# Modulation slices moved to other units, first value products by pairs of k-tiles, and gated attention scores by levels, in a hybrid transformer block

## The chip, the cores and the metric

The kernel runs on one core of one Trainium2 chip. The metric is the device time of one execution in microseconds (us); the median of several executions counts. One further execution was recorded by the hardware profiler; its trace is what the rows below come from. Engines are named as in the profile: PE is TensorE (matmuls), PEld its weight loads, DVE is VectorE, ACT is ScalarE, POOL is GpSimd, SP is SyncE, which issues most of the DMAs in program order.

## The reference, cut to what matters

One block over 512 tokens of width 1024, all in float32:

```
mod = silu(c) @ ada_w + ada_b                  # 1024 x 6144: shift1, scale1, gate1, shift2, scale2, gate2
h   = rmsnorm(x) * (1 + scale1) + shift1
gq, gk, gv, gr, g_lr, aq, ak, av, merge_a, merge_b = split(h @ w_in)
log_a = log_sigmoid(g_lr @ w2 + bias) / 16
# gated linear attention, 4 heads, dk 128, dv 256, chunks of 16 tokens
#   within a chunk: (q e^b)(k e^-b)^T, causal; across chunks: a state decayed by e^b_last
y_gla  = (rmsnorm(o_gla) * silu(gr)) @ w_gla
y_attn = dilated_attention(aq, ak, av) @ w_attn       # 12 heads of 64, rotary
x = x + gate1 * ((sigmoid(merge_a) * y_gla + sigmoid(merge_b) * y_attn) @ w_out)
h2 = rmsnorm(x) * (1 + scale2) + shift2
x = x + gate2 * (conv_ffn(h2) @ w_down)
out = rmsnorm(x)
```

## The kernel before, in words

**Products.** Every large product is made of three matmuls in a reduced float32 form: both operands are split into a high and a low part, and high x high, high x low and low x high are summed in PSUM (`three`, L1641). Weights come in units of 1 MB (`UNITS`, L95): two value units for the wide value heads (`vw`), six `qk`, `lr`, then for each of four heads `gqk`, `gv`, `gr`, then `ma`, `mb`, `wa`, `wg`, `wo`. Each unit is read by DMA into one of two slots of `raw`; ACT writes the high part (`split_hi`, L584), DVE the low part (`split_lo`, L1084), which frees the slot through the semaphore `raw_used`. A unit gives mostly two tiles of 128 x 512; the two PSUM banks 0 and 1 take turns by the position in `TILES`.

**Modulation.** shift1 and scale1 are needed first. `ada_in` holds their 8 MB in four quarters j; DVE sums 8 rows for each j (`ada_sums`, L1042), PE adds over the partitions with one-column matmuls (`shift_scale`, L1663), DVE makes the gain (`shift_and_gain`), ACT the high part of h (`high`) and DVE the low (`lower`). The other 16 slices (two groups r of 8) pass through the same two slots of `raw` as the weights, in the order of `RAW` (L125), and DVE adds each to `ada_acc` (`modulate`, L1110). When a group is summed, 16 one-column matmuls on 128-wide weights (`ada_part`, L1723) are strewn into one ordinary tile, named in `WITH_ADA`: group 0 in the second tile of the last `qk` unit, group 1 in the second tile of `gr` of head 2. The sums take a bank of their own in the alternation and DVE empties it (`ada_tile`).

**First products.** PE's order is written out at L1963: transposes of x, then the narrow value product (`first_hi`, `first_lo`, banks 0 and 1) and the wide one. The wide one takes k-tiles 0 to 3 together in `wide_hi(r)` after the third pair's modulation has begun, `wide_lo(k)` later, and k-tiles 4 to 7 at the very end, in `wide_rest`.

**Dilated attention.** While the second three `qk` units run, pieces of the attention of the first two heads are put between the tiles (`attention(p, i)`, PE L1797, DVE L1207). DVE also rotates each `qk` tile out of its bank (`rotate`, L1147), and SP carries the rotated halves to `qk` in eight DMAs (`shuffle`, L453), which stand in SP's queue between the weight loads, as do eight small copies of the gate weights (L493, L496).

**Gated attention.** For head h, steps `gla(h, i)` are put between the tiles of the next head. Step 0: PE sums the logs of the gates over chunks into two banks (128 columns and, in `side[1]`, 9 columns for each block of 128 tokens), ACT takes exponentials, DVE scales k and q. For each block b of 128 tokens DVE makes eight copies of the keys, each decayed up to one chunk further (`keys`, L1265: one copy of 128 x 1024 and eight multiplications in a row), and PE makes the scores from eight matmuls of 16 columns, each with its own copy as weights (`within`, L1842, L1852). `outputs` (L1856) then adds the values and the state.

Of the kernel before, what the change touches and what calls it, by code (L numbers as in the profile page):

```python
# [16 lines left out]
P = 128  # L17
# [37 lines left out]
C_KEEP = C_TRI + P + NCH + 1  # L55
# [18 lines left out]
def shape_constants():  # L74
# [6 lines left out]
    for n in range(NCH + 1):  # L81
        c[:, C_TRI + P + n] = np.where(row[:, 0] < CHUNK * n, -1.0 / 16.0, 0.0)
# [30 lines left out]
WITH_ADA = {(("qk", 1, 2), 1): 0, (("gr", 2, 0), 1): 1}  # L113
# [38 lines left out]
LATE = KT - 2  # L152
SPLIT_K = 5

def hybrid_block_kernel(nc, x, c, positions, ada_w, ada_b, norm1_w, w_in, gate_w2, gate_b, gla_norm_w,
# [3 lines left out]
    with ctx:  # L160
# [28 lines left out]
        def region(*places):  # L189
# [35 lines left out]
        q_in, k_in, gv, gr, logs, za, lrT, w2s, og_hi, og_lo, kk, at_sb, kt_sb, ke, state, eb, enb, ed, qB, o_sb, osq, ors = region(  # L225
# [4 lines left out]
            ("kk", 88, [P, NCH, P], F32), ("at_sb", 92, [P, 2, P], F32), ("kt_sb", 93, [P, 2, P], F32),  # L230
            ("ke", 94, [P, P], F32), ("state", 94.5, [P, DV], F32), ("eb", 95.5, [P, SEQ], F32),
            ("enb", 97.5, [P, SEQ], F32), ("ed", 99.5, [P, NB, NCH + 1], F32), ("qB", 99.75, [P, SEQ], F32),
            ("o_sb", 101.75, [P, 2, SEQ], F32), ("osq", 105.75, [P, 2, SEQ], F32), ("ors", 109.75, [P, SEQ], F32))

        vx_hi, vx_lo = region(("vx_hi", 16, [P, UE], F32R), ("vx_lo", 24, [P, UE], F32R))

# [63 lines left out]
        b_ps, gexp_done, qg_done, qB_done, kk_step, kk_done = (sem(n) for n in (  # L300
            "b_ps", "gexp_done", "qg_done", "qB_done", "kk_step", "kk_done"))
# [89 lines left out]
        def _(sp):  # L391
# [83 lines left out]
            for q in range(N_RAW):  # L475
# [5 lines left out]
                if q == 3:  # L481
# [3 lines left out]
                    sp.wait_ge(mod1_ps, KT // 2)  # L485
# [92 lines left out]
        def _(act):  # L578
# [91 lines left out]
            normed_out(4)  # L670
            normed_out(5)
            modulated(0)
            modulated(1)
            normed_out(6)
            normed_out(7)
            split_hi(1)
            for k in (2, 3):
                high(k)
            for k in (2, 3):
                modulated(k)  # L680
            for k in (4, 5):
                high(k)
            for k in (4, 5):
                modulated(k)
            split_hi(2)
            for k in (6, 7):
                high(k)

# [73 lines left out]
            def gla(h, i):  # L762

                if i == 0:
                    act.wait_ge(b_ps, h + 1)
                    if h > 0:
                        act.wait_ge(kk_done, NB * h)
# [3 lines left out]
                    act.activation(ed[:, :, :].rearrange("p b n -> p (b n)"), side[1][:, 0:NB * (NCH + 1)],  # L771
# [79 lines left out]
            for n in range(GROUPS):  # L851
                if n == 2:
                    split_hi(n + 1)
# [179 lines left out]
        def _(dve):  # L1033
# [8 lines left out]
            def ada_sums(j, half):  # L1042
# [4 lines left out]
                for k in range(half * KT // 2, (half + 1) * KT // 2):  # L1047
                    if k == 0:
                        dve.tensor_scalar(total, total, c_silu[:, 0:1], None, ALU.mult).then_inc(ada_step, 1)
                    else:  # L1050
                        dve.wait_ge(ada_step, KT * j + k)
# [58 lines left out]
            def modulate(n):  # L1110

                if n >= 2 * KT:
                    return
# [151 lines left out]
            def keys(h, b):  # L1265

                u = NB * h + b
                if u >= 1:
                    dve.wait_ge(at_ps, u)
                    dve.wait_ge(kk_done, u)  # L1270
                own = k_in[:, h % 2, b * P:(b + 1) * P]
                dve.tensor_copy(kk[:, :, :], own.rearrange("p (a n) -> p a n", a=1).broadcast_to((P, NCH, P))).then_inc(kk_step, 1)
                for n in range(NCH):
                    w = CHUNK * (n + 1)
                    decay = eb[:, b * P + w - 1:b * P + w]
                    dve.wait_ge(kk_step, NCH * u + n + 1)
                    dst = kk[:, n + 1, 0:w] if n < NCH - 1 else ke[:, :]
                    dve.tensor_scalar(dst, kk[:, n, 0:w], decay, None,
                                      ALU.mult).then_inc(kk_step if n < NCH - 1 else kk_done, 1)

            def gla(h, i):

                if i == 0:
# [9 lines left out]
                    keys(h, 0)  # L1293
                    chunks = q.rearrange("p (b n c) -> p b n c", b=NB, n=NCH)
                    start = ed[:, :, 0:NCH].rearrange("p b (n o) -> p b n o", o=1).broadcast_to((P, NB, NCH, CHUNK))
                    dve.tensor_tensor(qB[:, :].rearrange("p (b n c) -> p b n c", b=NB, n=NCH), chunks, start,
                                      ALU.mult).then_inc(qB_done, 1)
                if 2 <= i <= 5:
# [7 lines left out]
                    if b + 1 < NB:  # L1306
                        keys(h, b + 1)
                if 3 <= i <= 5:
                    b = i - 3
                    dve.wait_ge(p3_done, NB * h + b + 1)  # L1310
                    new = side[1][:, 64:64 + DV]
# [4 lines left out]
                    else:  # L1316
                        dve.wait_ge(st_done, 3 * h + b)
                        ins = dve.scalar_tensor_tensor(state[:, :], state[:, :], ed[:, b, NCH:NCH + 1], new,
# [56 lines left out]
            split_lo(0)  # L1375
            ada_sums(1, 0)
# [4 lines left out]
            split_lo(1)  # L1381
            ada_sums(2, 0)
            ada_sums(2, 1)
            lower(2)
            lower(3)
            shift_and_gain(2)
            ada_sums(3, 0)
            ada_sums(3, 1)
            lower(4)
            lower(5)  # L1390
            shift_and_gain(3)
            for k in (6, 7):
                modulate_late(k)
            for k in (6, 7):
                lower(k)
            split_lo(2)
            modulate(0)

            def evac_wide():
# [795 lines left out]
```

## Time and profile before

| | |
|---|---|
| median of 3 executions | 958.49 us (958.16 to 959.00) |
| profiled execution, its own time | 959.86 us |
| its span, first to last instruction | 958.1 us |
| instructions | 12161 |
| PE busy | 920.2 us (96%) |
| DVE busy | 527.1 us (55%) |
| ACT busy | 372.7 us (39%) |

The span is what the trace shows; the time of the execution holds 1.8 us more around it. The profiled execution is 1.4 us over the median. In rows of instructions the columns are start, duration, engine, line of the code, operation, tiles written and read, shapes and count; in square brackets is how long the engine stood idle before and what ended it. A matmul of plain float32 is recorded as two instructions, one in the reduced form as one.

### The profile page before, as it was taken

How to read it: one execution, taken by the hardware profiler on the slowest of the kernel's cores; microseconds unless marked ns; L12 is line 12 of the kernel's file. 1: busy time of each engine (PE TensorE's matmuls, PEld its weight loads, DVE VectorE, ACT ScalarE, POOL GpSimd, SP SyncE). 2: the span in 40 equal slices, each digit the busy share in tenths (PEclk: the TensorE clock that was granted, in tenths of full speed). 3: DMA queues.
4: the chain of work that ended last, by engine and by line, in shares of the span. 5: the costliest groups of instructions: out<-in, count | busy, mean ns of one | idle time of the engine just before them, and what ended most of it. 6: DMA issues, size and time to landing. Idle time of an engine off the chain costs nothing.

```text
span 958.1 us, 12161 instructions
## 1 busy us (share of the span) xinstructions
PE 920.2 (96%) x4733; PEld 781.5 (82%) x4733; DVE 527.1 (55%) x687; ACT 372.7 (39%) x461; POOL 35.9 (4%) x33
## 2 busy tenths in 40 slices
PE   3899999999999999999999999999999999999996
PEld 3887787889989898888888788888888888888885
DVE  5877893775756365653254466555555555433223
ACT  5451112568443334625223335343333433422225
POOL 0010000000000000000002120000000000000003
PEclk9999996999999999999999999999999999999999
DMA  9947844723441212122222442333343333322302
GB/s 312 382 133 224 245 113 111 241 89 105 160 132 45 75 59 75 58 88 75 101 88 88 176 114 63 88 88 88 107 112 88 88 88 104 116 88 99 120 0 88
DMA packets 114270, 112.87 MB, mean 118 GB/s; under 512 B 4676, under 2 KB 104390, under 8 KB 111927
## 3 DMA queue, kind: packets, MB, share of 16 engines
q1 hardware_dynamic: 113511, 110.16, 36.7%
q10 hardware_dynamic: 720, 2.16, 0.6%
q8 instruction: 28, 0.46, 0.2%
q14 instruction: 11, 0.09, 0.0%
HBM read 104.77 MB, written 4.19 MB: 114 GB/s over the span
## 4 chain that ended last, share of the span: by engine, by line
PE 84%; DVE 6%; DMA 3%; ACT 2%; SPq 2%; issue 2%; DVEq 0%; ACTq 0%
PE bank L1644 23%; PE bank L1646 23%; PE bank L1645 23%; PE bank L1852 2%; DMA raw<-in_w_in_dram 2%; PE bank L2106 1%; ACT w_hi L593 1%; SPq L461 1%; PE bank L1727 1%; DVE w_lo L1092 1%; DMA x<-x_spill 1%; PE bank L1939 1%; PE bank L1793 1%; PE bank L1873 1%; PE bank L1766 1%
## 5 line engine op out<-in xcount | busy, mean ns | idle before, releaser
L1644 PE MATMUL bank<-h_hi,w_hi 128*128 128x512 f32 x672 | 269.1, 400 | 8.2 <-DVE w_lo L1092 5.2
L1646 PE MATMUL bank<-h_hi,w_lo 128*128 128x512 f32 x672 | 263.6, 392 | 0.0
L1645 PE MATMUL bank<-h_lo,w_hi 128*128 128x512 f32 x672 | 263.2, 392 | 0.0
L1644 PEld LDWEIGHTS bank<-h_hi,w_hi 128*128 128x128 f32 x672 | 127.3, 189 | 35.8 <-issue 8.8
L1646 PEld LDWEIGHTS bank<-h_hi,w_lo 128*128 128x128 f32 x672 | 127.1, 189 | 27.0
L1645 PEld LDWEIGHTS bank<-h_lo,w_hi 128*128 128x128 f32 x672 | 127.3, 189 | 25.4 <-issue 0.2
L1092 DVE TENSOR_TENSOR w_lo<-raw,w_hi 128x2048 fp32r<-128x2048 f32 (+2 forms) x46 | 85.6, 1872 | 60.8 <-ACT w_hi L593 56.1
L1099 DVE TENSOR_TENSOR w_lo<-raw,w_hi 128x2048 fp32r<-128x2048 f32 x31 | 71.1, 2292 | 86.3 <-ACT w_hi L601 86.3
L1598 DVE SCALAR_TENSOR_TENSOR conv<-bank,vecs,conv 128x511 f32<-128x511 f32 x88 | 65.7, 748 | 65.8 <-ACT conv L984 60.3
L593 ACT ACTIVATE w_hi<-raw 128x2048 fp32r<-128x2048 f32 (+2 forms) x44 | 71.7, 1644 | 60.3 <-DMA raw<-in_w_in_dram 52.0
L601 ACT ACTIVATE w_hi<-raw 128x2048 fp32r<-128x2048 f32 x31 | 59.1, 1905 | 69.3 <-PE bank L1646 69.3
L984 ACT ACTIVATE conv<-bank,vecs 128x512 f32<-128x512 f32 x44 | 34.1, 778 | 104.7 <-PE bank L1646 104.7
L1644 PE MATMUL bank<-hs_hi,w_hi 128*128 128x512 f32 x176 | 68.6, 390 | 0.0
L1646 PE MATMUL bank<-hs_hi,w_lo 128*128 128x512 f32 x176 | 68.5, 389 | 0.0
L1645 PE MATMUL bank<-hs_lo,w_hi 128*128 128x512 f32 x176 | 68.5, 389 | 0.0
L1646 PEld LDWEIGHTS bank<-hs_hi,w_lo 128*128 128x128 f32 x176 | 33.0, 188 | 6.9
L1644 PEld LDWEIGHTS bank<-hs_hi,w_hi 128*128 128x128 f32 x176 | 33.0, 188 | 6.9
L1645 PEld LDWEIGHTS bank<-hs_lo,w_hi 128*128 128x128 f32 x176 | 33.0, 188 | 6.7
L1644 PE MATMUL bank<-w_hi,h_hi 128*128 128x256 f32 x128 | 36.5, 285 | 0.1
L1645 PE MATMUL bank<-w_lo,h_hi 128*128 128x256 f32 x128 | 36.2, 283 | 0.0
L1646 PE MATMUL bank<-w_hi,h_lo 128*128 128x256 f32 x128 | 36.2, 283 | 0.0
L1125 DVE SCALAR_TENSOR_TENSOR ada_acc<-raw,c_silu,ada_acc 128x2048 f32<-128x2048 f32 x14 | 32.9, 2347 | 3.1 <-DMA raw<-in_ada_w_dram 2.9
(267 smaller groups left out, 1345.1 us busy)
## 6 DMA issues: line engine op xcount, KB each, us to landing
raw<-in_w_up_dram SPq DMA_DIRECT2D x44, 512.0 KB, 4.7
raw<-in_w_in_dram SPq DMA_DIRECT2D x19, 1024.0 KB, 5.2
raw<-in_ada_w_dram SPq DMA_DIRECT2D x16, 1024.0 KB, 5.5
raw<-in_w_down_dram SPq DMA_DIRECT2D x22, 512.0 KB, 3.6
raw<-in_w_in_dram SPq DMA_DIRECT2D x20, 512.0 KB, 5.2
ada_in<-in_ada_w_dram SPq DMA_DIRECT2D x16, 512.0 KB, 9.6
raw<-in_w_gla_branch_dram SPq DMA_DIRECT2D x4, 1024.0 KB, 4.9
raw<-in_w_out_dram SPq DMA_DIRECT2D x4, 1024.0 KB, 6.2
```

Source lines behind the costliest of these rows:

```text
L461: sp.dma_start(qk[32 * half:32 * half + 32, g, a // 2, a % 2, :], rope[32 * a:32 * a + 32, j % 2, half, :]).then_inc(qk_in[j % 2], 16)
L593: last = act.activation(hv, r, ACT.Copy)
L601: act.activation(w_hi[:, slot, :], raw[:, slot, :], ACT.Copy).then_inc(hi_done, 1)
L984: act.activation(conv[:, s, t, :], bank[2 * (1 - s) + t][:, :], ACT.Identity, scale=vecs[:, bass.ds(i + (V_CW2 + t * FT), 1)], bias=vecs[: ...
L1092: last = dve.tensor_tensor(lv, r, hv.bitcast(F32), ALU.subtract)
L1099: dve.tensor_tensor(w_lo[:, slot, :], raw[:, slot, :], w_hi[:, slot, :].bitcast(F32), ALU.subtract).then_inc(raw_used, 1)
L1125: ins = dve.scalar_tensor_tensor(ada_acc[:, :], src, c_silu[:, k:k + 1], ada_acc[:, :], ALU.mult, ALU.add)
L1598: ins = dve.scalar_tensor_tensor(conv[:, s, t, tap:SEQ], src[:, 0:SEQ - tap], vecs[:, bass.ds(i + (col + t * FT), 1)], conv[:, s, t, tap:S ...
L1644: pe.matmul(out_ap, wh, xh, start=first, stop=False, skip_group_check=True)
L1645: pe.matmul(out_ap, wh, xl, start=False, stop=False, skip_group_check=True)
L1646: return pe.matmul(out_ap, wl, xh, start=False, stop=last, skip_group_check=True)
L1852: pe.matmul(side[2][0:m, at:at + CHUNK], kk[:, n, 0:m], q_in[:, h % 2, b * P + at:b * P + at + CHUNK], start=True, stop=True, skip_group_c ...
```

## The change

1. The 16 late slices of the modulation are tied to other units (`ADA_UNITS`): the first three `qk`, then `gqk`, `gv`, `gr` of head 1, `gqk`, `gv` of head 2, all three of head 3, the four `ma` and the first `mb`. `WITH_ADA` moves too: group 0 goes into the second tile of `gr` of head 2, group 1 into the second tile of the last `mb`; `ada_tile(0)` and `ada_tile(1)` move with them.
2. The first products go in quarters of two k-tiles: `quarter_hi(j)` (narrow and wide, both high parts), `shift_scale(j + 1)`, `quarter_lo(j)`. `wide_rest` is gone. The first six transposed tiles stand ahead of `shift_scale(0)` instead of four. In quarter 1 the last of the eight rows isn't summed by DVE; PE multiplies it by the column of `c_silu` (`DIRECT`). The splits of the units 1, 2 and 3 stand earlier on ACT and DVE, and SP's order of loads is another: both value units ahead of the second quarter of `ada_in`, the spill of x after the load of unit 3.
3. The eight decayed key copies of each block are replaced by scaled copies made once for each head (`scaled_copies`): seven broadcast multiplications by factors from 45 columns of chunk sums for each block, instead of 9. Scores of a block: two matmuls over every second chunk (the even ones with the keys as they are, the odd ones with `mixed` keys), two on pairs of 32 columns, one on a half of 64 columns, five in place of eight.

```diff
-WITH_ADA = {(("qk", 1, 2), 1): 0, (("gr", 2, 0), 1): 1}
+WITH_ADA = {(("gr", 2, 0), 1): 0, (("mb", 3, 0), 1): 1}
+ADA_UNITS = ([("qk", 0, g) for g in range(GROUPS)] + [(kind, 1, 0) for kind in ("gqk", "gv", "gr")]
+             + [("gqk", 2, 0), ("gv", 2, 0)] + [(kind, 3, 0) for kind in ("gqk", "gv", "gr")]
+             + [("ma", u, 0) for u in range(4)] + [("mb", 0, 0)])
+ADA_AT = {UNIT[u]: n for n, u in enumerate(ADA_UNITS)}
 for _n in range(N_UNITS):
     RAW.append(("w", _n))
-    if _n == 2:
-        RAW.append(("ada", 0))
-    if _n == 3:
-        RAW += [("ada", 1), ("ada", 2)]
-    if 4 <= _n <= 2 * KT:
-        RAW.append(("ada", _n - 1))
+    if _n - 1 in ADA_AT:
+        RAW.append(("ada", ADA_AT[_n - 1]))
...
-            for j in range(KT // 2):
-                if j in (1, 2):
-                    load(j - 1)
-                load_first(j)
+            load_first(0)
+            load(0)
+            load(1)
+            load_first(1)
+            load_first(2)
             load(2)
+            load_first(3)
+            load(3)
             sp.wait_ge(xn_sb, KT)
             sp.dma_start(x_spill, xn[:, :, :].rearrange("p k n -> p (k n)")).then_inc(spilled, 16)
-            load(3)
...
+            def scaled_copies(h):
+                q, k = in_chunks(q_in[:, h % 2, :]), in_chunks(k_in[:, h % 2, :])
+                half = NCH // 2
+                dve.tensor_tensor(in_chunks(mixed[:, :]), k, factors(F_MIX, NCH), ALU.mult).then_inc(scaled_done, 1)
+                dve.tensor_tensor(in_chunks(k32[:, :]), k, factors(F_K32, NCH), ALU.mult).then_inc(scaled_done, 1)
+                dve.tensor_tensor(k64[:, :, :].rearrange("p b (n c) -> p b n c", c=CHUNK), k[:, :, 0:half, :],
+                                  factors(F_K64, half), ALU.mult).then_inc(scaled_done, 1)
+                for o in range(2):
+                    dve.tensor_tensor(q32[:, :, o, :].rearrange("p b (n c) -> p b n c", c=CHUNK),
+                                      q[:, :, 4 * o + 2:4 * o + 4, :], factors(F_Q32 + 2 * o, 2),
+                                      ALU.mult)
+                dve.tensor_tensor(q64[:, :, :].rearrange("p b (n c) -> p b n c", c=CHUNK), q[:, :, half:NCH, :],
+                                  factors(F_Q64, half), ALU.mult).then_inc(scaled_done, 2)
+                dve.tensor_tensor(in_chunks(ke[:, :]), k, factors(F_KE, NCH), ALU.mult).then_inc(scaled_done, 1)
+                dve.tensor_tensor(in_chunks(qB[:, :]), q, factors(F_QB, NCH), ALU.mult).then_inc(qB_done, 1)
...
-                for n in range(NCH):
-                    at = CHUNK * n
-                    m = (at + CHUNK + 31) // 32 * 32
-                    pe.matmul(side[2][0:m, at:at + CHUNK], kk[:, n, 0:m], q_in[:, h % 2, b * P + at:b * P + at + CHUNK],
-                              start=True, stop=True, skip_group_check=True)
-                pe.transpose(side[3][:, 0:P], ke[:, :], ident).then_inc(at_ps, 1)
+                blk = slice(b * P, (b + 1) * P)
+                queries = q_in[:, h % 2, blk].rearrange("p (n e c) -> p e n c", e=2, c=CHUNK)
+                at = side[2][:, 0:P]
+                at_chunks = at.rearrange("p (n e c) -> p e n c", e=2, c=CHUNK)
+                for e, own in enumerate((k_in[:, h % 2, blk], mixed[:, blk])):
+                    pe.matmul(at_chunks[:, e], own, queries[:, e], start=True, stop=True, skip_group_check=True)
+                for o in range(2):
+                    m, col = 32 + 64 * o, 32 + 64 * o
+                    pe.matmul(at[0:m, col:col + 32], k32[:, b * P:b * P + m], q32[:, b, o, :], start=True, stop=True,
+                              skip_group_check=True)
+                pe.matmul(at[0:P // 2, P // 2:P], k64[:, b, :], q64[:, b, :], start=True, stop=True, skip_group_check=True)
+                pe.transpose(side[3][:, 0:P], ke[:, blk], ident).then_inc(at_ps, 1)
...
+            def quarter_hi(j):
+                for k in (2 * j, 2 * j + 1):
+                    first_hi(k)
+                for k in (2 * j, 2 * j + 1):
+                    wide_hi(k)
+            def quarter_lo(j):
+                for k in (2 * j, 2 * j + 1):
+                    first_lo(k)
                 for r in range(NB):
+                    for k in (2 * j, 2 * j + 1):
+                        last = wide_lo(r, k)
...
-            for k in range(4):
+            for k in range(6):
                 normed_tile(k)
             shift_scale(0)
-            for k in range(4, KT):
+            for k in (6, 7):
                 normed_tile(k)
-            first_hi(0)
-            first_hi(1)
+            quarter_hi(0)
             shift_scale(1)
...
+            quarter_lo(0)
+            quarter_hi(1)
             shift_scale(2)
+            quarter_lo(1)
+            quarter_hi(2)
             shift_scale(3)
+            quarter_lo(2)
+            quarter_hi(3)
             pe.wait_ge(cst_in, 16)
...
-            wide_rest()
+            quarter_lo(3)
```

## Rows read from the trace of the kernel before

**Rows 1.** The page: busy time by engine, and granted clock in 40 slices
```profile
PE 920.2 (96%) x4733; PEld 781.5 (82%) x4733; DVE 527.1 (55%) x687; ACT 372.7 (39%) x461; POOL 35.9 (4%) x33
PEclk9999996999999999999999999999999999999999
```
**Rows 2.** PE's waits over the whole span: total us, times, longest us
```profile
PE bank L1644 <- DVE w_lo L1092: 5.2, 3, 2.0
PE bank L1668 <- DVE ada_in L1052: 3.6, 1, 3.6
PE bank L1644 <- DVE rope_t L1162: 2.4, 2, 2.2
PE bank L1644 <- DVE mod L1140: 0.7, 1, 0.7
```
**Rows 3.** Windows: length, busy time and count by engine, granted clock, DMA share, GB/s
```profile
32.00:35.40 3.40, 3.40 (x18) 3.27 (x17) 3.33 (x4) 2.92 (x4) 0.00 (x0) 0.50 1.10 348
...
145.00:147.30 2.30, 0.08 (x2) 0.03 (x1) 2.30 (x5) 0.03 (x1) 0.00 (x0) 1.00 0.51 82
...
149.00:161.00 12.00, 12.00 (x43) 10.55 (x43) 0.00 (x0) 2.21 (x8) 0.00 (x0) 0.50 0.60 154
```
**Rows 4.** Timeline of PE, 19 to 72 us
```profile
19.46 1.84 PE L1668 MATMUL bank<-ones,ada_in 128*128 128x1 f32 x8
...
30.53 1.02 PE L1668 MATMUL bank<-ones,ada_in 128*128 128x1 f32 x8 [3.63 <-DVE ada_in L1052]
...
47.87 4.03 PE L1946 MATMUL bank<-w_hi,h_lo 128*128 128x512 f32 x16
...
71.04 0.47 PE L1644 MATMUL bank<-h_hi,w_hi 128*128 128x512 f32 x1 [1.67 <-DVE w_lo L1092]
```
**Rows 5.** Groups by shape, 0 to 560 us: busy us, mean ns
```profile
L1092 DVE TENSOR_TENSOR w_lo<-raw,w_hi 128x2048 fp32r<-128x2048 f32 x29 | 66.4, 2290 | 49.8 <-ACT w_hi L593 45.1 <-DMA x<-x_spill 4.7
L1125 DVE SCALAR_TENSOR_TENSOR ada_acc<-raw,c_silu,ada_acc 128x2048 f32<-128x2048 f32 x14 | 32.9, 2347 | 3.1 <-DMA raw<-in_ada_w_dram 2.9
L1052 DVE SCALAR_TENSOR_TENSOR ada_in<-ada_in,c_silu 128x512 f32<-128x512 f32 x28 | 21.1, 752 | 1.4
L1296 DVE TENSOR_TENSOR qB<-q_in,ed 128x512 f32<-128x512 f32 x4 | 2.7, 684 | 0.0
L848 ACT ACTIVATE sB<-bank 128x512 f32<-128x512 f32 x8 | 4.8, 596 | 22.9 <-PE bank L1646 22.9
```
**Rows 6.** The chain that ended last, 84 to 103 us: start, us, what
```profile
84.50 0.58 SPq L433
...
97.76 5.38 DMA raw<-in_w_in_dram
```
**Rows 7.** Timeline of PE around both groups of one-column matmuls, and 277 us
```profile
147.30 0.47 PE L1644 MATMUL bank<-h_hi,w_hi 128*128 128x512 f32 x1 [2.22 <-DVE rope_t L1162]
...
277.31 0.58 PE L1644 MATMUL bank<-h_hi,w_hi 128*128 128x512 f32 x1
...
316.70 0.72 PE L1727 MATMUL bank<-ones,ada_acc 128*128 128x1 f32 x6
317.29 0.48 PE L1644 MATMUL bank<-h_hi,w_hi 128*128 128x512 f32 x1
```
**Rows 8.** The scores of one block on PE, and their weight loads by width
```profile
250.90 1.52 PE L1852 MATMUL bank<-q_in,kk 128*32 128x16 f32 x16
252.27 0.31 PE L1854 MATMUL bank<-cst,ke 128*128 128x128 f32 x1
...
L1852 PEld LDWEIGHTS bank<-q_in,kk 128*128 128x128 f32 x64 | 8.4, 192 | 0.0
...
L1852 PEld LDWEIGHTS bank<-q_in,kk 128*32 128x32 f32 x64 | 3.2, 110 | 6.0 <-issue 5.5
```
**Rows 9.** Timeline of DVE, 262 to 272 us
```profile
263.49 2.28 DVE L1092 TENSOR_TENSOR w_lo<-raw,w_hi 128x2048 fp32r<-128x2048 f32 x1
...
268.88 2.00 DVE L1278 TENSOR_SCALAR kk<-kk,eb 128x16 f32<-128x16 f32 x7
```

More of the change, by code:

```diff
@@ L80, in shape_constants @@
     c[:, C_TRI:C_TRI + P] = np.where(same & (row <= col), -1.0 / 16.0, 0.0)
-    for n in range(NCH + 1):
-        c[:, C_TRI + P + n] = np.where(row[:, 0] < CHUNK * n, -1.0 / 16.0, 0.0)
+    spans = [(0, n) for n in range(NCH + 1)]
+    spans += [(n, n + 1 - n % 2) for n in range(NCH)]
+    spans += [(n, 2 * (n // 2) + 2) for n in range(NCH)]
+    spans += [(n, NCH) for n in range(NCH)]
+    spans += [(n, NCH // 2) for n in range(NCH // 2)]
+    spans += [(2 * (n // 2), n) for n in (2, 3, 6, 7)]
+    spans += [(NCH // 2, n) for n in range(NCH // 2, NCH)]
+    for n, (first, end) in enumerate(spans):
+        c[:, C_TRI + P + n] = np.where((row[:, 0] >= CHUNK * first) & (row[:, 0] < CHUNK * end), -1.0 / 16.0, 0.0)
     c[:, C_KEEP:C_KEEP + P] = col >= row
@@ L152 @@
 LATE = KT - 2
+DIRECT = {1: KT - 1}
+ADA_STEPS = [KT - (j in DIRECT) for j in range(KT // 2)]
 SPLIT_K = 5
@@ L669, in _ @@
             high(1)
-            normed_out(4)
-            normed_out(5)
+            split_hi(1)
+            for k in range(4, KT):
+                normed_out(k)
             modulated(0)
             modulated(1)
-            normed_out(6)
-            normed_out(7)
-            split_hi(1)
             for k in (2, 3):
@@ L1263, in gates, with factors @@
                     dve.tensor_tensor(logs[:, b, :], logs[:, b, :], z_abs_sb[b], ALU.add).then_inc(logs_done, 1)
[L1265 to L1272, printed above, removed]
-                for n in range(NCH):
[L1274 to L1279, printed above, removed]
+            def factors(at, count):
+                return ed[:, :, at:at + count].rearrange("p b (n o) -> p b n o", o=1).broadcast_to((P, NB, count, CHUNK))
@@ L1495, in _ @@
                 if u == 0:
+                    modulate(UNIT[("mb", u, 0)])
                     for i in (8, 9):
                         gla(3, i)
+            ada_tile(1)
             for b in range(NB):
@@ L1663, in shift_scale @@
             def shift_scale(j):
-                pe.wait_ge(ones_set, 1)
-                pe.wait_ge(ada_step, KT * (j + 1))
-                for n in range(4):
-                    last = pe.matmul(bank[7][:, 4 * j + n:4 * j + n + 1], ada_rows(j, 0)[:, n * P:(n + 1) * P], ones[:, 0:1],
-                                     start=True, stop=True, skip_group_check=True)
+                for rows, moving, first in ((DIRECT.get(j), c_silu, True), (0, ones, False)):
+                    if rows is None:
+                        continue
+                    if first:
+                        pe.wait_ge(silu_done, 1)
+                        pe.wait_ge(ada_landed[2 * j + 1], 32)
+                        pe.wait_ge(mod_done, j)
+                    else:
+                        pe.wait_ge(ones_set, 1)
+                        pe.wait_ge(ada_step, sum(ADA_STEPS[:j + 1]))
+                    for n in range(4):
+                        last = pe.matmul(bank[7][:, 4 * j + n:4 * j + n + 1], ada_rows(j, rows)[:, n * P:(n + 1) * P],
+                                         moving[:, rows:rows + 1], start=(n == 0 and (first or j not in DIRECT)),
+                                         stop=not first, skip_group_check=True)
                 last.then_inc(mod1_ps, 1)
@@ L1878, in outputs @@
                 if b < NB - 1:
-                    last = pe.matmul(side[1][:, 64:64 + DV], kt_sb[:, u % 2, :], gv[:, h % 2, b, :],
+                    last = pe.matmul(side[1][:, DV:2 * DV], kt_sb[:, u % 2, :], gv[:, h % 2, b, :],
                                      start=True, stop=True, skip_group_check=True)
@@ L1930, in first_lo @@
                         last.then_inc(acc_ready, 1)
-            def wide_hi(r):
-                pe.wait_ge(raw_used, 2)
-                pe.wait_ge(xn_sb, KT)
-                for k in range(KT // 2):
-                    pe.wait_ge(hh_done, k + 1)
-                    for v in (w_hi, w_lo):
-                        pe.matmul(side[1 + r][:, :], h_hi[:, k, r::DIL], v[:, 1, 2 * k * UW:2 * (k + 1) * UW],
-                                  start=(k == 0 and v is w_hi), stop=False, skip_group_check=True)
@@ L1963, in _, with wide_weights, wide_hi @@
-            for k in range(4):
+            def wide_weights(k):
+                j = k % (KT // 2)
+                two = slice(2 * j * UW, 2 * (j + 1) * UW)
+                return (w_hi[:, 1, two], w_lo[:, 1, two]) if k < KT // 2 else (vx_hi[:, two], vx_lo[:, two])
+            def wide_hi(k):
+                unit = UNIT[("vw", k // (KT // 2), 0)]
+                for part, v in enumerate(wide_weights(k)):
+                    if part == 0:
+                        pe.wait_ge(hi_done, unit + 1)
+                    else:
+                        pe.wait_ge(raw_used, RAW_AT[("w", unit)] + 1)
+                    for r in range(NB):
+                        if k == 0 and part == 0:
+                            pe.wait_ge(xn_sb, KT - NB + r + 1)
+                        pe.matmul(side[1 + r][:, :], h_hi[:, k, r::DIL], v,
+                                  start=(k == 0 and part == 0), stop=False, skip_group_check=True)
```

121 lines of the change are left out of this document (45 added, 76 removed).

## The prediction

> **What bounds the kernel now.** I read the page first: PE is busy for 96% of the span, DVE for 55%, and only one slice of the clock row is low, the seventh [rows 1]. So time can come from three places: work that PE no longer does, PE's waits, and stretches at a low clock. Next PE's waits: behind the first 20 us they are few and they all lie before 150 us or are small [rows 2]. 5.2 us are waits for the low part of weights, 3.6 us one wait for DVE's sums of the modulation, 2.4 us waits for a bank that `rotate` must empty, 0.7 us for the bank of group 1. From 150 us to the tail PE hardly waits, so there only its own instructions count. Last the windows by clock: PE ran at 0.5 (1.2 GHz, not 2.4) from 32.0 to 35.4 us, and from about 148.0 to 165.1, of which 149 to 161 stands in the rows [rows 3]. PE was busy throughout both, so half of each was lost: 1.7 us and 8.5 us (17.1 / 2). Before the first it had stood idle for 3.6 us and then run only one-column matmuls [rows 4]; before the second it had run tiny matmuls from 144.2 us and then stood idle to 147.3 [rows 3, 7].
>
> **Part 1, the modulation slices.** (a) The second low stretch began behind a 2.2 us wait for the bank of the tile before, which arises because group 0's sums sit in the alternation: the second tile of the last `qk` needs the bank that its first tile just filled, and DVE, with a slice of 2.35 us [rows 5] ahead of it, came late [rows 7]. After the change neither the sums nor that slice stand there; the tile takes the bank rotated one tile earlier. I take the wait and the 8.5 us of the clock as gone. What else could bring the drop is the small matmuls of the attention alone, under 1 us a piece between dense tiles.
> (b) The waits for weights. From 71.0 to 147.3 us PE waited 2.05, 1.46, 0.16 and 2.22 us, 5.9 in all; 1.67 more stands at 71.0 and is counted in part 2. The first goes: `raw` no longer takes three slices ahead of the second `qk` unit, whose weights are then split some 10 us sooner. The second stays: from 84.5 to 97.8 us the chain runs through SP's own queue, one load, eight small copies, one slice, eight shuffles, then the next load [rows 6], and none of these is taken out. Counted forward in the new order, the load leaves SP 12.6 us after the one ahead of it, lands 5.4 us later, and two splits of 2.0 and 2.4 us end 1.7 us after PE wants them. About 0.5 us more for DVE, whose attention pieces then set the pace. So 5.9 - 2.2 = 3.7 us; between 1 (DVE late again) and 5.9.
> (c) The sums themselves cost the same at full clock: 3 matmuls are 6 instructions in 0.59 us [rows 7], twice 3 us before and after. Group 0 now stands where group 1 stood, with the same 0.7 us [rows 2]. Group 1 goes into the last `mb` unit, where nothing lies between the two tiles: the second needs the bank of the first, so PE waits until ACT has emptied it, 0.6 us [rows 5] and the signals, together 0.9 us (0.6 to 1.3). That is a new loss. The next tile waits for `ada_tile(1)`, 0.2 us of work, done while the last two k-tiles of `mb` run.
> (d) Eleven slices are now added beside the gated attention and `ma`, each 2.35 us on DVE, each a load of 1 MB in the same two slots. What is behind them on DVE is the split and the masks. The cover: the low part of a unit ends at 265.8 us and PE begins with it at 277.3, 11.5 us later [rows 7, 9]. One more slice and its landing (5.4 us) are 7.8 us, under that. DVE also loses the key copies of part 3. So nothing.
>
> **Part 2, the first products.** PE's matmuls stay the same, 0.24 us each for 512 columns (16 in 4.03 us) and 0.12 for 256. What moves is when the modulation is ready. Eight transposes now stand ahead of `shift_scale(0)`, 0.21 us each, so the first gain comes 1.7 us later, at about 23.4 us. DVE then makes two low parts (2.3 us each, the second waiting 1.2 us for ACT), to 29.2 us, and seven of the eight rows of quarter 1, 0.5 + 6 x 0.79, to 34.4; before they ended at 30.5 [rows 4, 5]. By then PE has done the first narrow and wide high parts, ready at 32.1 us. From 34.4 on PE has three groups of one-column matmuls (3 x 0.8 and 0.2 more for the first), four low parts of 2.9 us, three high parts of 5.7 and 0.4 of transposes: 31.7 us, to 66.1. DVE's chain for quarters 2 and 3 (splits, eight sums, two lower parts, about 9.5 us a quarter against PE's 9.4) delays it by 0.3. So the first `qk` tile starts at 66.4 instead of 71.0 us [rows 4]: its weights are then split since 60 us, and the wait of 1.67 us goes. That is 4.6 us. But between 32.1 and 35.4 us PE is idle or on one column, 3.3 us; the second low stretch followed 3.1 us of that kind, while waits of 1.5 to 2.1 us between dense tiles changed nothing. So I count a new stretch at 1.2 GHz as long as the first one, 3.4 us, which costs 1.7, partly in place of DVE's waits: 3.0 us gained. Bounds: 1 us (DVE or the landing of `ada_in` later than I think) and 5.5. Taking one row from DVE is worth 0.75 us, in the sum already; PE makes its extra matmuls while it waits.
>
> **Part 3, the scores.** A block takes 1.37 us now, 16 instructions from 250.90 to 252.27 [rows 8]. Their moving columns are only 16; the weight loads lengthen from 110 to 192 ns between 32 and 128 columns, 0.85 ns a column [rows 8]. At that rate the 1280 columns of weights of a block are 1.09 us and the rest, 0.28, are starts and changes of width. The new block has 2 x (128 + 128 + 32 + 96 + 64) = 896 columns, 0.77 us, and the same rest: 1.05. In proportion it would be 0.96. I take 1.0, so 0.37 less, 16 times: 5.9 us. The scores are no better than before by 2.4 us if every change of width costs 0.1 more, and 7.7 us better if only one is paid. The 45 columns in place of 9 ride on weight loads of 128 columns, nothing; ACT's exponential of 180 instead of 36 columns lies beside PE. The rate of columns says otherwise by a page of the Trainium skill ("TensorE: Matmul & The Clock Gate", back-to-back issue gap): a matmul of N columns takes N / 2.4 + 2.5 ns. By that the block goes from 0.15 to 0.24 us and the part loses 1.5 us instead of winning 5.9; at 16 columns the trace does not agree, 86 ns an instruction against 9. DVE's keys, 0.7 + 2.0 + 0.3 us a block [rows 9], 48 us in all, become some 3.4 us of broadcast products a head, priced by the row of `qB`, 0.68 for 512 columns [rows 5]. DVE was not waited for here, so nothing. The new copies are all due before the first block: at 287.6 us DVE began the step, 1.4 + 4.1 us puts them at 293.1, and PE wants them at 297.9. Covered by 4.8 us.
>
> **Sum.** 8.5 + 3.7 - 0.9 + 3.0 + 5.9 = 20.2 us. From the profiled execution's own 959.9 that is 939.7; it stands 1.4 over the median of 958.5, so 938.3; I say 938.
>
> **Rivals.** (A) The clock falls again around the attention pieces at 130 to 160 us, whatever is done about group 0: DVE's masks still stand there and PE stops for them once for 2 us. Then 8.5 us are not won: 946.5. For it: DVE was busy nearly without a break from 120 us. Against: 7 us of slices leave that stretch. (B) The first quarter keeps its clock and the scores go by the cheap bound: 1.7 + 1.8 more, and up to 2 of waits: 933. (C) The scores win little, strided query columns or changes of width eating it: 942 to 944. (D) The first products win nothing, since DVE's sums of quarter 1 end 4 us later than before: 941. (E) Slower than before: the slices in the gated stage hold the two slots, so weights are late at every unit with a slice. It decides once a slice holds its slot 11.5 us longer than now; against 7.8 us counted. To lose the 20.2 us won, thirteen units would each have to stop PE for 1.6 us: 960 or more. The same place speaks for it in the `qk` stage, where PE did wait 5.2 us for weights; there, though, shuffles stood in SP's queue, here none. (F) No change: needs A, C and D together and more.
>
> **How the numbers follow.** My forecast, 935 to 941.5: 0.60. B, 931 to 935: 0.14. C or D, 941.5 to 944.5: 0.12. A, 944.5 to 950: 0.09. E 0.03, F 0.01, better than 931 0.01. The range of 931 to 945 holds about 0.87 by these cases. Faster by over 0.2% (1.9 us, what a measurement of this kernel can tell from no change) 0.96, within it 0.01, slower 0.03.
>
> **What would show it.** In the changed kernel: the windows from 145 to 165 us at clock 1.00; the first dense tile of `qk` near 66 to 68 us with no wait; one wait of 1 to 2 us at the fourth `qk` unit; about 1.0 us from the first score matmul of a block to the transpose; one new wait of 0.9 us at the last `mb`; no wait for weights behind 150 us. Wrong it would be if the clock row shows a low slice again, or PE waits for `w_lo` beside the gated attention.

## The result, and the profile after

The changed kernel takes **942.62 us**, median of four executions (941.0 to 944.0), the kernel before 958.75 beside it: a ratio of 0.983, 95% interval 0.982 to 0.984. The forecast was 938, range 931 to 945. The profiled execution has a span of 940.8 us where it was 958.1: 17.3 us less, and the sum said 20.2. The page after, its PE row and its granted clock, which answer to [rows 1]:

```profile
PE 913.7 (97%) x4645; PEld 773.0 (82%) x4645; DVE 496.5 (53%) x570; ACT 372.9 (40%) x461; POOL 35.9 (4%) x33
...
PEclk9899999999999999999999999999999999999998
```

The seventh slice is no longer low; the second has lost a little. PE's waits that bear on the change, which answer to [rows 2] (total us, times, longest us):

```profile
PE bank L1951 <- DVE w_lo L1109: 1.7, 1, 1.7
PE bank L1661 <- ACT sB L867: 0.8, 1, 0.8
PE bank L1661 <- DVE mod L1158: 0.7, 1, 0.7
PE bank L1693 <- DVE ada_in L1069: 0.5, 1, 0.5
PE bank L1661 <- DVE w_lo L1109: 0.4, 1, 0.4
```

The 5.2 us for weights are 0.4, the 3.6 us for DVE's sums of the modulation 0.5, the 2.4 us for `rotate` are gone. New are 0.8 us behind ACT, the bank in `mb`, and 1.7 us in the first high parts, for the low part of a unit; that one belongs to the execution as much as to the change, since e2 and e6 below show 2.2 and 1.7 us there with the old order, and e5 0.8 with the new one. The windows, which answer to [rows 3]:

```profile
23.80:27.20 3.40, 3.40 (x16) 3.40 (x17) 2.28 (x2) 3.40 (x6) 0.00 (x0) 0.50 1.09 386
34.00:37.40 3.40, 3.40 (x12) 2.86 (x11) 3.29 (x6) 3.37 (x5) 0.00 (x0) 0.50 1.09 382
149.00:161.00 12.00, 12.00 (x83) 10.90 (x82) 7.74 (x7) 5.47 (x8) 0.00 (x0) 1.00 0.65 196
```

The long low stretch is gone (83 matmuls in those 12 us, 43 before). There are two short ones in the first products, 23.8 to 27.2 us and 34.0 to 37.4, where I counted one; one stood there before. And PE's timeline, at the first `qk` tile, a block of scores with the dense matmul ahead of it, and the last `mb` tile:

```profile
66.19 0.39 PE L1661 MATMUL bank<-h_hi,w_hi 128*128 128x512 f32 x1
...
227.47 0.28 PE L1663 MATMUL bank<-w_hi,h_lo 128*128 128x256 f32 x1
227.59 0.33 PE L1880 MATMUL bank<-q_in,k_in 128*128 128x64 f32 x2
227.75 0.39 PE L1880 MATMUL bank<-q_in,mixed 128*128 128x64 f32 x2
228.07 0.53 PE L1883 MATMUL bank<-q,enb 128*32 128x32 f32 x4
228.53 0.33 PE L1885 MATMUL bank<-q,k 128*64 128x64 f32 x2
228.79 0.33 PE L1886 MATMUL bank<-cst,ke 128*128 128x128 f32 x1
...
447.12 0.47 PE L1661 MATMUL bank<-h_hi,w_hi 128*128 128x512 f32 x1 [0.78 <-ACT sB L867]
```

The first `qk` tile begins at 66.19 us (71.04 in [rows 4]). A block of scores lasts from 227.59 to 228.79, 1.20 us instead of 1.37 [rows 8].

**Where the time went, by stages.** The starts of four kinds of matmul on PE cut the span: the first `qk` tile, the first sum of the gates' logs, the first product on `oa_hi`, the end. Stage lengths in us, each from one trace; the other kernels are the experiments below:

| kernel | to the first `qk` | `qk` | gated, `ma`, `mb` | from `oa` to the end |
|---|---|---|---|---|
| before | 71.04 | 166.77 | 240.72 | 479.54 |
| after | 66.19 | 148.41 | 241.71 | 484.48 |
| e2, scores alone | 70.67 | 167.01 | 237.03 | 484.33 |
| e3, slices alone | 70.12 | 148.19 | 245.45 | 479.19 |
| e4, slices and scores | 69.60 | 147.84 | 241.72 | 484.62 |
| e5, after with 128 bytes | 66.19 | 148.58 | 241.58 | 479.09 |
| e6, before with 128 bytes | 72.64 | 166.71 | 240.48 | 484.43 |

The last column is the surprise: from `oa` on, PE makes the same 2162 matmuls in both kernels, and yet the stage is 4.9 us longer. The trace shows it in the rate of matmuls. The same 90 us of the `down` stage, first in the kernel before, then in the changed one (length, PE busy and count, clock, DMA share, GB/s):

```profile
830.00:920.00 90.00, 90.00 (x399) 1.00 0.26 94
```

```profile
830.00:920.00 90.00, 90.00 (x388) 1.00 0.19 70
```

PE is busy throughout at full clock in both, but 388 matmuls are done where 399 were. The starts in the trace are 226.7 ns apart in the kernel before, and 229 and 238 in turn, 233.3 on average, in the changed one. The groups by shape say the same, the `down` stage after (busy us, mean ns; 389 or 390 before):

```profile
L1661 PE MATMUL bank<-hs_hi,w_hi 128*128 128x512 f32 x176 | 69.6, 395 | 0.0
L1663 PE MATMUL bank<-hs_hi,w_lo 128*128 128x512 f32 x176 | 69.5, 395 | 0.0
L1662 PE MATMUL bank<-hs_lo,w_hi 128*128 128x512 f32 x176 | 69.5, 395 | 0.0
```

Matmuls that follow each other without a wait are called dense. Below, "the excess" is the sum over neighbouring dense matmuls of 512 columns (those under 300 ns apart) of their distance less 226.7 ns: 1.7 us before, 7.7 after.

### The profile page after: what moved, and what is told of

Read it like the earlier page. It is cut to its first block, busy times and chain, and to the rows that moved or that the text cites. A ratio compares the mean times of both kernels' runs of the same rounds, so it can differ in the third digit from the quotient of the medians.

```text
span 940.8 us, 11854 instructions
## 1 busy us (share of the span) xinstructions
PE 913.7 (97%) x4645; PEld 773.0 (82%) x4645; DVE 496.5 (53%) x570; ACT 372.9 (40%) x461; POOL 35.9 (4%) x33
## 4 chain that ended last, share of the span: by engine, by line
PE 90%; DVE 2%; ACT 2%; DMA 2%; SPq 2%; issue 1%; DVEq 0%; ACTq 0%
PE bank L1661 25%; PE bank L1663 24%; PE bank L1662 24%; PE bank L1981 1%; PE bank L2137 1%; DMA x<-x_spill 1%; PE bank L1883 1%; PE bank L1781 1%; PE bank L1905 1%; PE bank L1819 1%; PE bank L1986 1%; PE bank L1776 1%; PE bank L1792 1%; PE bank L1880 1%; PE bank L1753 1%
## 5 line engine op out<-in xcount | busy, mean ns | idle before, releaser
L1327 DVE COPY_PREDICATED at_sb<-cst,bank 128x128 f32<-128x128 uint32 x16 | 4.8, 302 | 53.8 <-PE bank L1886 53.8
```

## The experiments

Each kernel was measured with the kernel before beside it, in three groups on three chips: e1 to e4, e5 to e8, and e9 to e12. The kernel before took 959.46, 959.5 and 958.77 us there, so times of different groups compare to within about 1 us. Stage lengths and excess come from one trace each.

**e1, the changed kernel again,** without an edit.

> The changed kernel again, without an edit. In its trace PE's dense 512-column matmuls began 232.5 ns apart from 448.8 to 588.0 us and 233.3 ns apart in the whole down stage, at clock 1.00, against 226.7 elsewhere and in the kernel before; that costs some 6 us. Theory 1, the wider pitch belongs to the program (where its instructions lie, or what ran before them): the same two stretches come back at the same pitch, and the time is 941 to 944 us. Theory 2, it belongs to the one execution: the pitch is 226.7 ns there, or other stretches are wide, and the times of the rounds scatter by 3 us or more, the fastest near 937 us.

Measured 942.48 us (941.6 to 942.88), excess 7.6 us, the same stretches wide to within 2 us of where they began. So it belongs to the program, not to the execution. The stretch from 448.8 us that the expectation names begins 7.5 us ahead of `oa`; there the starts lie behind the wait in `mb`, and e5 below, which is fast afterwards, has them at 231 to 232 ns too. They are no part of the effect.

**e2, the scores alone; e3, the slices alone; e4, both.** The kernel before with the edits of that part of the diff and no others. In e3, for example, its core:

```diff
-WITH_ADA = {(("qk", 1, 2), 1): 0, (("gr", 2, 0), 1): 1}
+WITH_ADA = {(("gr", 2, 0), 1): 0, (("mb", 3, 0), 1): 1}
...
-                        modulate(n)
...
-                        ada_tile(1)
+                        ada_tile(0)
...
+                modulate(UNIT[("ma", u, 0)])
```

> The kernel before with part 3 alone (the scores by levels, the scaled copies, the 45 columns of chunk sums). My forecast of the part was 16 x 0.37 = 5.9 us. The traces of before and after show a block of 1.37 and 1.20 us, which makes 2.7 us. Theory 1, the part is worth what the block shows: 955.8 us (955 to 956.5). Theory 2, the keys taken off DVE also help PE, since the masks come earlier: 952 to 954. Rival, it is worth nothing or the clock changes elsewhere: 958 or more. If the wide pitch of after comes with this part, its down stage begins instructions 233 ns apart and 3.5 us of it are lost again: near 959.

> The kernel before with part 1 alone (the slices at other units, group 0 in gr of head 2, group 1 in the last mb), the order of the first products as it was. My terms: 8.5 for the low clock gone + 3.7 to 5.5 for waits in the qk stage - 0.9 for the wait in mb = 11.3 to 13.1, so 945.4 to 947.2 us. Rival, the low stretch at 148 us stays away only when DVE is also relieved of the first products' order: 954 to 956 and a low slice in the clock row. If the wide pitch of after comes with the sums in mb, it shows here too, from 449 us on, and costs 5 to 6 us: 951 to 953.

> Parts 1 and 3 together, without part 2 (first products as before). If the parts add: e3's time less 2.7 us, so 942.7 to 944.5 us without the wide pitch, and after is 1.9 to 3.7 us ahead of it by part 2 (my term: 3.0) less what the wide pitch takes. If this kernel is as fast as after, or faster, part 2 wins nothing in the end, or brings the wide pitch with it. Where the trace shows 226.7 ns in the down stage here and 233 in after, part 2 moves the instructions into it; where both are wide, it is part 1 or 3.

Measured, beside 959.46 for the kernel before on the same chip: e2 960.37 (ratio 1.0006, 0.9994 to 1.0017), e3 944.73 (0.9846, 0.9825 to 0.9867), e4 945.4 (0.9848, 0.9829 to 0.9866). The slices alone bring 14.7 us, and the long low stretch is gone with them (e3, 150 to 160 us, clock 1.00), so part 2 isn't needed for that:

```profile
150.00:160.00 10.00, 10.00 (x69) 9.03 (x68) 5.64 (x6) 6.83 (x11) 0.00 (x0) 1.00 0.72 208
```

The scores alone bring nothing, although their stage is 3.7 us shorter (240.72 to 237.03, and 245.45 to 241.72): the excess is 7.8 us in e2 and e4, 1.8 in e3. So the wide matmuls come with part 3. In e2 they set in at the first product on `oa_hi`; before it the starts are 0.23 us apart in the rows, behind it 0.22 to 0.24, on average 232.7 ns over the 47 distances on `oa` against 227.4 in the kernel before:

```profile
474.25 0.39 PE L1663 MATMUL bank<-h_lo,w_hi 128*128 128x512 f32 x1
474.48 0.39 PE L1664 MATMUL bank<-h_hi,w_lo 128*128 128x512 f32 x1
474.71 0.40 PE L1662 MATMUL bank<-oa_hi,w_hi 128*128 128x512 f32 x1
474.94 0.39 PE L1663 MATMUL bank<-oa_lo,w_hi 128*128 128x512 f32 x1
475.16 0.40 PE L1664 MATMUL bank<-oa_hi,w_lo 128*128 128x512 f32 x1
475.40 0.39 PE L1662 MATMUL bank<-oa_hi,w_hi 128*128 128x512 f32 x1
```

**e5 and e6, 128 bytes more** behind the constants, in the changed kernel and in the kernel before:

```diff
+        pad = sb("pad", [P, 32])
         ones = sb("ones", [P, P])
```

> The changed kernel with one unused tensor of 128 bytes a partition behind the constants, so that every tensor behind them lies 256 bytes further than in the kernel before, where they lay 128 bytes further. Theory 1, the wide pitch (232.5 to 233.3 ns) comes from where the moving operand lies against the weights: with the old place modulo 256 bytes the pitch is 226.7 ns again in the stages of oa, og, mix and hs, the sum of excess over 226.7 ns falls from 7.6 to under 3 us, and the time is 936.5 to 938 us. Theory 2, it comes from where the instructions lie (the program of PE is unchanged here, word for word in its order): the pitch stays wide and the time stays 942.5.

> The kernel before with the same 128 bytes, and nothing else. Theory 1, place of the operands: the down stage and the stages of oa, og and mix go wide (232 to 233 ns), and the time rises by 5 to 6 us, to 964 to 965 us. Theory 2, place of the instructions: no change, 959 to 960 us.

Measured, beside 959.5: e5 **936.54** (936.29 to 937.35; ratio 0.9764, 0.9751 to 0.9777), excess 1.6 us, and 399 matmuls in the window:

```profile
830.00:920.00 90.00, 90.00 (x399) 1.00 0.19 70
```

e6 963.47 (ratio 1.0040, 1.0026 to 1.0054), excess 7.8 us. An unused tensor takes 5.9 us from the one kernel (from e1, measured on another chip; in the trace 5.4, from `oa` to the end) and adds 4.0 to the other (in the trace 4.9). The window of e6:

```profile
830.00:920.00 90.00, 90.00 (x387) 1.00 0.26 94
```

PE's program is the same in each pair, so the place of its instructions is ruled out.

**e9, everything 128 bytes further,** on top of e5 and e8 (below):

```diff
+        front = sb("front", [P, 32])
         raw = sb("raw", [P, 2, UE])
```

> The changed kernel with the 128 bytes and group 1's sums in wg (936.2 us), and 128 bytes more in front of everything: weights and moving operands all lie 128 bytes further modulo 256, so their distance is as before. Theory 1, what counts is the distance between weights and moving operand: no change, 935.5 to 937 us, excess over 226.7 ns near 1.6 us. Theory 2, it is the moving operand's own place modulo 256 (the fast ones lay at 128, the slow ones at 0): now all of the 3090 dense matmuls go wide, some 6 ns each, which is 15 us and more: 950 us or over. The edges of both: if only the stages change in which one of the two moved, the third reading (the weights' own place) is as good as theory 2 and stays open.

Measured 935.27 us (934.72 to 935.88), beside 958.77 for the kernel before; excess 1.5. Weights and moving operands now all lie at 0 modulo 256, and no stage from `qk` on is wide. With the `up` units, where only the weights had moved, neither operand's own place explains it: what counts is the distance between the two.

**e11 and e12, other distances,** on top of e5 and e8, with 48 and with 40 floats in the unused tensor in place of 32:

> As the kernel with group 1 in wg (936.2 us), but with 192 bytes in place of 128 behind the constants: oa, og, mix and hs lie 64 bytes off the weights modulo 256 (128 off was the slow place, 0 the fast one). If any place but that of the weights is slow: wide pitch in those stages and 941 to 942 us. If only 128 bytes off is slow: 226.7 ns and 936 to 937. Between the two if the pitch grows with the distance: about 939.

> As the kernel with group 1 in wg, with 160 bytes behind the constants: those tensors lie 32 bytes off the weights modulo 256. If any other place is slow: 941 to 942 us; if the pitch grows with the distance: 937 to 938; if only 128 bytes off is slow: 936 to 937.

Measured: at 64 bytes 938.99 (937.87 to 939.17), excess 4.0; at 32 bytes 942.69 (941.39 to 943.6), excess 7.7, as at 128. e8, at 0, has 936.23 and 1.6. So it doesn't grow with the distance: 0 is best, 64 about half as bad, 32 and 128 equally bad. At 64 bytes the three products of a triple differ, in e11 (830 to 920 us):

```profile
L1662 PE MATMUL bank<-hs_hi,w_hi 128*128 128x512 f32 x132 | 52.0, 394 | 0.0
L1664 PE MATMUL bank<-hs_hi,w_lo 128*128 128x512 f32 x132 | 51.7, 392 | 0.0
L1663 PE MATMUL bank<-hs_lo,w_hi 128*128 128x512 f32 x131 | 50.8, 388 | 0.0
```

The first `up` units of e11 have the 64 bytes in the other direction (the weights further on), and there nothing is saved: the starts are 233.4 ns apart, as at 128. First e11, then e9 (560 to 612 us):

```profile
L1662 PE MATMUL bank<-h_hi,up_hi 128*128 128x512 f32 x16 | 6.3, 395 | 0.0
```

```profile
L1663 PE MATMUL bank<-h_hi,up_hi 128*128 128x512 f32 x16 | 6.2, 390 | 0.0
```

**e7 and e10, why a block of scores is dearer than I said.** e7 takes adjacent query columns, on top of e5; e10 takes equal widths, on top of e8. Both compute other scores than the block needs and stand for their time alone. The edits that matter here:

```diff
-                queries = q_in[:, h % 2, blk].rearrange("p (n e c) -> p e n c", e=2, c=CHUNK)
+                queries = q_in[:, h % 2, blk].rearrange("p (e n c) -> p e n c", e=2, c=CHUNK)
...
-                at_chunks = at.rearrange("p (n e c) -> p e n c", e=2, c=CHUNK)
+                at_chunks = at.rearrange("p (e n c) -> p e n c", e=2, c=CHUNK)
```
```diff
-                    pe.matmul(at[0:m, col:col + 32], k32[:, b * P:b * P + m], q32[:, b, o, :], start=True, stop=True,
+                    pe.matmul(at[:, col:col + 32], k32[:, blk], q32[:, b, o, :], start=True, stop=True,
...
-                pe.matmul(at[0:P // 2, P // 2:P], k64[:, b, :], q64[:, b, :], start=True, stop=True, skip_group_check=True)
+                pe.matmul(at[:, P // 2:P], k32[:, blk], q64[:, b, :], start=True, stop=True, skip_group_check=True)
```

> As the changed kernel with the 128 bytes, but the two wide score matmuls of a block read and write 64 adjacent columns instead of every second chunk of 16; this changes which scores are computed, the masks and all the rest stay. A block takes 1.20 us with every second chunk. Theory 1, the moving columns stand in chunks and that is what makes a block dearer than my 1.0 us: 1.0 to 1.05 us a block and 2.4 to 3 us off the time of the kernel with the bytes alone. Theory 2, the price of a small matmul grows with its moving columns (64 and 32 against 16): the block stays at 1.2 us and the time within 0.5 us.

> As the kernel with group 1 in wg (936.2 us), but the three narrow score matmuls load weights of 128 columns in place of 32, 96 and 64, so a block loads 1280 columns of weights and never changes width; this changes which scores are computed. A block takes 1.20 us with 896 columns. Theory 1, the changes of width cost (128 to 32: 205 ns, 96 to 64: 179, 64 to 128: 152, against 112 between equal loads of 128): ten steps of 112 ns, 1.10 to 1.15 us a block, and the time falls by up to 1.5 us. Theory 2, my rate of 0.85 ns a column with a fixed rest: 1280 columns are 1.37 to 1.5 us a block, and the time rises by 2.7 to 4.5 us.

e7: 936.72 us against 936.54, the gated stage 241.57 against 241.58: strided columns cost nothing. e10: 933.48 (933.0 to 934.02) where e8 has 936.23 and e9, which has e8's order and was measured beside it, 935.27, so 1.8 us less; the gated stage 233.82 against 236.85 in both, and a block in its timeline:

```profile
227.52 0.33 PE L1881 MATMUL bank<-q_in,k_in 128*128 128x64 f32 x2
227.69 0.39 PE L1881 MATMUL bank<-q_in,mixed 128*128 128x64 f32 x2
227.91 0.58 PE L1884 MATMUL bank<-q,enb 128*128 128x32 f32 x4
228.33 0.41 PE L1886 MATMUL bank<-q,enb 128*128 128x64 f32 x2
228.58 0.28 PE L1887 MATMUL bank<-cst,ke 128*128 128x128 f32 x1
```

1.06 us with 1280 columns of weights, 1.20 with 896. The changes of width cost more than the columns saved; theory 2 is out, and the gain is above what theory 1 gave.

**e8, group 1's sums in the first tile of `wg`,** on top of e5 (`ada_tile(1)` moves with it), where four matmuls of the standard deviations stand ahead of it:

```diff
-WITH_ADA = {(("gr", 2, 0), 1): 0, (("mb", 3, 0), 1): 1}
+WITH_ADA = {(("gr", 2, 0), 1): 0, (("wg", 0, 0), 0): 1}
```

> As the changed kernel with the 128 bytes, but group 1's sums ride in the first tile of wg instead of the second tile of the last mb, DVE takes them out ahead of the wg tiles. Theory 1, the wait of 0.78 us in mb is hidden by the four matmuls of the standard deviations that PE makes between wa and wg, so 0.7 us less than the kernel with the bytes alone. Rival, the wait only moves (the bank of the last wa tile must be emptied by DVE, which is slower there): the same time within 0.3 us, or up to 1 us more.

936.23 us against 936.54 for e5 on the same chip: in the trace the wait of 0.78 us is gone and the span is 0.8 shorter, but the times of the two overlap (935.55 to 936.88, 936.29 to 937.35), so the gain isn't shown in them.

## Why the prediction was right, and where it was not

The forecast was on the right side and in its range. The trace bears out most of the mechanisms; that the number is only 4.6 us off is in part luck, since terms erred both ways and one was missing. The forecast's own case, 935 to 941.5, was missed: 942.62 lies in the band from 941.5 to 944.5, which had 0.12 and stood for C or D. D did not happen, C took 2.2 us, and the larger part, 4.9, had no case. Working against these were 1.8 us more for waits, 1.3 without a name, 1.1 for an early start, 0.7 more in the first products and 0.1 in `mb`.

- **8.5 us for the clock: right.** 149 to 161 us runs at 1.00; e3 shows that the slices alone do it. Rival A is out. I did not separate the bank's wait from DVE's lighter load; that the wait set off the drop is argued from the order in the trace alone.
- **3.7 us for waits in `qk`: too low.** 5.9 us became 0.4, so 5.5. The step that failed is "the second stays": the load behind SP's copies did come late, but PE waited 0.38 us instead of 1.7, at 99.39 us, the fourth `qk` unit. The load left SP 12.4 us after the one ahead of it (76.2 and 88.6 us) and landed 5.6 us later, near the 12.6 and 5.4 counted, and the splits ended at 99.25 us; what was off is when PE comes to them, at 99.0. The `qk` stage is 18.4 us shorter: 3.1 for the sums that left it, 8.5, 5.5, and 1.3 in small pieces that I can't name.
- **-0.9 us in `mb`: right,** 0.78.
- **3.0 us for the first products: right.** The first `qk` tile came at 66.19 us, forecast at 66.4 + 1.7; of the 4.85 us won, 1.1 is that this execution received its first rows earlier (the first transpose at 11.66 us, not 12.77), so 3.7. Without part 2, e4 takes 2.9 us more than e1, the changed kernel beside it. The new low stretch that I charged with 1.7 us came (34.0 to 37.4), and another ahead of it. But the time at low clock in the first 40 us differs between the traces, from 3.4 us (before, e4, e5) to 6.8 (after, e2, e3, e8) and over (e6, 6.8 there and 3.4 more at 56), with either order; so that term can't be read from one trace, and the times, 2.9 us, decide. Rival D is out.
- **5.9 us for the scores: mis-sized, 3.7 in the stage.** From a block's first score to its transpose it is 1.21 us instead of 1.37, 2.6 us in the 16 blocks where 5.9 were counted. The failing step is "the same rest", 0.28 us for starts and changes of width. In the trace of before the widths rise within a block, 32, 64, 96, 128; in the new block they jump, and from the trace's starts a step from 128 to 32 takes 205 ns, from 96 to 64 179, from 64 to the next 128 152, against 112 between loads of 128. With 0.83 ns a column (32, 58, 85 and 112 ns between starts at 32 to 128 columns) the rest was 0.30 us and became 0.46. The other 1.1 us lie at the edges of the blocks, which the term left out. The dense matmul ahead of a block has 128 columns of weights; before, the first score had 32 and came 209 ns later, now it has 128 and comes after 120 (227.47 to 227.59), 1.4 us in 16 blocks; the step from the transpose back to dense matmuls gives 0.3 of it back. The row of before that shows the edge, with 250.90 in [rows 8]:

```profile
250.69 0.28 PE L1646 MATMUL bank<-w_hi,h_lo 128*128 128x256 f32 x1
```

So a price on each change of width, rival C's mechanism, is what the term lacked, and e10 bears it out. The bound given for it doesn't follow from its price: four changes at 0.1 in 16 blocks are 6.4 us, which would leave nothing of 5.9, and not 2.4. The 1.5 us of loss by the Trainium skill ("TensorE: Matmul & The Clock Gate", back-to-back issue gap) rests on a formula that the section gives for an isolated matmul; it says itself that the formula counts too little at few columns where each matmul has its own weight load, and it puts 1 to 64 columns at about 60 cycles, some 25 ns. The traces have 32 to 112 ns between such instructions, by the width of the weights, and the block became shorter.
- **DVE's copies: covered.** PE never waits for them.
- **Slices in the gated stage: covered, as argued.** No wait for weights behind 150 us. Rival E is out. The count of eleven slices there is too low, the list in `ADA_UNITS` has thirteen behind the `qk` units; the argument goes by single units and stands.
- **Missing: the place of the tensors, 5.4 us** (484.48 against 479.09 from `oa` to the end in e5; 5.9 in the times of e1 and e5). No step of mine looked at what a larger constant does to the addresses behind it. I had costed the 45 columns at nothing.

Against the 20.2: 8.5 and 5.5, 1.3 unnamed, -0.8, 3.7 and 1.1 for the early start, 3.7 for the scores, are 23.0; less 4.9 for the place of the tensors (484.48 against 479.54 before) 18.1. The span lost 17.3; the 0.8 left stands in the gated stage, which got 1.0 longer where 3.1 for the sums, 0.8 of wait and -3.7 make 0.2.

## What to carry to other kernels

When a tensor's size changes, look at what is allocated behind it: compare the count of matmuls in equal windows of a stage that the change does not touch. If it fell at full clock, put the tensors back to their old place modulo 256 bytes against the weights; an unused tensor of 128 bytes was worth more here than the whole rebuilt score product. And small matmuls are priced by the changes of width between them as much as by their columns: count the transitions, not only the sum.

The fastest kernels that do the whole computation were e9, 935.27 us (ratio to the kernel before 0.9752, 0.9738 to 0.9765), and e8, 936.23 (0.9759, 0.9746 to 0.9772): the changed one with the tensors aligned and group 1 in `wg`. Between these two and e5 the intervals overlap, so none is shown to be the fastest.

## What the runs showed of the hardware that was not expected

- The distance between a dense matmul's moving operand and the weights in SBUF, taken modulo 256 bytes, sets its pace in a stream of weight loads and matmuls of 128x512, at full clock in the `down` stage: 226.7 ns at 0 (before, e3, e5, e9), 229 on average with the moving operand 64 bytes further (e11), 233.3 at 32 (e12) and at 128 (after, e2, e4, e6). With the weights 64 bytes further it is 233.4 (the first `up` units of e11). Modulo 512 the distance is 0 in the kernel before and 256 in e5, and both are fast; 128 is slow. Other residues were not tried.
- The Trainium skill ("TensorE: Matmul & The Clock Gate", step-by-step: what each phase is for) says that the moving operand and the weight loads have read ports of their own, so that loading the next weights takes no bandwidth from the running matmul. These runs do not agree in full: up to 6.6 ns a matmul depend on how the two lie to each other. Which part of the path they meet in, the runs don't show.
- Behind some waits of PE the same matmuls are about 231 ns apart for up to nine of them before 226.7 returns (before, 84.2 and 328.9 us; after, 99.4), behind others not (before, 71.0 and 107.7). The cause was not tested.
- Of small float32 matmuls, a pair with 128-wide weights costs the same with 64 query columns in four chunks, read and written, as with 64 adjacent ones (e7, gated stage 241.57 against 241.58 us).
